# Attention shares weigh the values with the values stationary, two heads in the two column halves of TensorE

## The reference, cut to what matters

```
s = q[lo:hi] @ k[:hi].T * scale          (+ masks; fox: + forget biases; mla: + rotary part)
p = softmax(s)
o = p @ v[:hi]                            one head: 128 queries x 64 channels
y = concat(o over 16 heads) @ w_out       then residual and layer norm
```

## Time and profile before

| what | value |
|---|---|
| three runs, median (lowest to highest) | 2730.32 us (2729.82 to 2733.73) |
| the profiled execution: its span | 2727.5 us (first to last instruction; no separate time is given for it, the median is 2.8 us longer) |
| busy: PE, PEld, DVE, ACT, POOL | 97%, 83%, 37%, 51%, 72% |
| chain that ended last, by engine | PE 89%, DVE 6%, ACT 2%, DMA 1% |
| TensorE's mean granted clock | 0.991 of 2.4 GHz |

### The profile page before, as it was taken

The page is one execution under the profiler, slowest core; times in us unless marked ns, Lnnn a source line. Parts: engine busy times, 40 slices in busy tenths (PEclk is TensorE's granted clock), DMA queues, the critical chain, the costliest instruction groups (busy, mean ns, idle before and its releaser), DMA issues.

```text
span 2727.5 us, 35975 instructions
## 1 busy us (share of the span) xinstructions
PE 2651.0 (97%) x15016; PEld 2269.8 (83%) x15016; DVE 1017.6 (37%) x1695; ACT 1386.9 (51%) x1666; POOL 1972.7 (72%) x432
## 2 busy tenths in 40 slices
PE   6999989999999999999999999999999999999998
PEld 4889977899888778888888888888888888877887
DVE  6868867543212452121124311212441121244312
ACT  3754544555544555454454544544544454445543
POOL 3767764787887738878875688887658878774885
PEclk8999989999999999999999999999999999999999
DMA  8869843555554526546553455554425555443553
GB/s 331 309 230 353 311 157 108 191 213 182 200 193 175 181 88 223 188 170 216 186 197 137 160 186 194 192 192 177 155 111 199 192 193 192 179 179 115 194 192 108
DMA packets 80390, 521.78 MB, mean 191 GB/s; under 512 B 8908, under 2 KB 9292, under 8 KB 24420
## 3 DMA queue, kind: packets, MB, share of 16 engines
q1 hardware_dynamic: 72884, 492.72, 49.9%
q10 hardware_dynamic: 7344, 26.74, 2.5%
HBM read 518.38 MB, written 1.05 MB: 190 GB/s over the span
## 4 chain that ended last, share of the span: by engine, by line
PE 89%; DVE 6%; ACT 2%; DMA 1%; issue 0%; POOL 0%; SPq 0%; DVEq 0%; ACTq 0%
PE acc L555 17%; PE acc L594 17%; PE mb L532 11%; PE cb L532 11%; PE cb L507 10%; PE cb L534 6%; PE mb L534 6%; PE mb L647 2%; PE acc L872 1%; DVE hT L1875 1%; PE acc L507 1%; PE cb L833 1%; PE mb L857 1%; PE cb L647 1%; ACT whi L1184 1%; DMA raw<-in_w 1%
## 5 line engine op out<-in xcount | busy, mean ns | idle before, releaser
L2512 POOL TENSOR_TENSOR wlo<-raw,whi 128x2048 fp32r<-128x2048 f32 x428 | 1972.5, 4621 | 731.4 <-ACT whi L1184 667.3
L1184 ACT ACTIVATE whi<-raw 128x2048 fp32r<-128x2048 f32 x428 | 818.4, 1915 | 582.5 <-PE cb L532 251.3
L555 PE MATMUL acc<-whi,ARR 128*128 128x512 f32 x1312 | 366.5, 391 | 0.0
L532 PE MATMUL cb<-hT,whi 128*128 128x512 f32 x1280 | 335.4, 393 | 0.0
L532 PE MATMUL mb<-hT,whi 128*128 128x512 f32 x1280 | 334.1, 393 | 0.1
L555 PEld LDWEIGHTS acc<-whi,ARR 128*128 128x128 f32 x1312 | 245.6, 188 | 53.0 <-issue 2.9
L507 PE MATMUL cb<-hT,whi 128*128 128x256 f32 x1536 | 281.1, 285 | 0.0
L594 PE MATMUL acc<-whi,hT 128*128 128x512 f32 x960 | 270.8, 390 | 8.7 <-DVE hT L1875 7.4
L532 PEld LDWEIGHTS mb<-hT,whi 128*128 128x128 f32 x1280 | 230.2, 189 | 43.9 <-issue 3.1
L532 PEld LDWEIGHTS cb<-hT,whi 128*128 128x128 f32 x1280 | 229.6, 189 | 40.5
L1944 DVE TENSOR_TENSOR cb<-cb,AR 128x512 f32<-128x512 f32 x80 | 56.0, 700 | 552.8 <-ACT AR L1192 552.7
(11 more groups left out here) (332 smaller groups left out, 3367.6 us busy)
## 6 DMA issues: line engine op xcount, KB each, us to landing
raw<-in_w SPq DMA_DIRECT2D x436, 1024.0 KB, 4.8
AR<-in_a ACTq DMA_DIRECT2D x35, 512.0 KB, 6.2
AR<-in_a SPq DMA_DIRECT2D x29, 512.0 KB, 5.7
z<-in_a ACTq DMA_DIRECT2D x16, 512.0 KB, 6.8
gb<-in_lng SPq DMA_DIRECT2D x12, 512.0 KB, 5.7
gb<-in_lnb SPq DMA_DIRECT2D x12, 512.0 KB, 6.5
gb<-in_normg SPq DMA_DIRECT2D x8, 512.0 KB, 7.6
x<-in_x SPq DMA_DIRECT2D x1, 1024.0 KB, 8.4
```

Source lines behind the costliest of these rows:

```text
L532: ins = pe.matmul(to[j], wh[:, w], hT[:, k, :], start=k == 0, stop=k == 7)
L555: ins = pe.matmul(acc[:, 2 * t + c, 0:c1 - c0], xs[y], a[:, kk * width + c0:kk * width + c1], start=first and kk == 0 and m == 0, stop=las ...
L1184: ac.activation(whi[i % NH][:, :], raw[u % NR][:, :], ACT.Copy).then_inc(*up(s_hi, ("hi", i)))
L2512: po.tensor_tensor(wlo[i % NH][:, :], raw[(i + NADA) % NR][:, :], whi[i % NH][:, :].bitcast(F32), ALU.subtract).then_inc(*up(s_lo, ("lo", i)))
```

## The change

The stationary operand and the moving one trade places in weigh: the values of one head (128 keys x 64 channels) are loaded, and the turned shares (128 keys x 128 queries) move. The result has channels in the partitions; the two heads o = 0, 1 of a pair of items go to output partitions 0 to 63 and 64 to 127, that is, to the two column halves of the array. So weigh now takes two items at once, and the sum is already turned. The row sums are now what is turned: DVE takes reciprocals and spreads them over 64 columns a head into `OS` ("share"), PE turns that (turn_sums), ACT copies it back to `OS`, DVE multiplies the accumulator with it ("scale"), ACT writes the high part and DVE the low part ("split"). The order in tail is written anew. On PE, "scale" and "split" are nothing; on ACT and DVE they stand in the list where the list has them.

```diff
@@ -410,7 +410,10 @@
             t, h0 = order[name][i]
             same = [j for j in pv_order(name) if order[name][j][0] == t and order[name][j][1] // 8 == h0 // 8]
-            return same[-1] == i
+            return same[-2] == i
+
+        def exps_of(name, t, g):
+            return [i for i in range(16) if order[name][i][0] == t and order[name][i][1] // 8 == g]
         def steps(name):
@@ -424,21 +427,32 @@
         started = {"dsa0": 11, "dsa1": 11, "fox": 18, "mla": 9}
-        weighed_early = {"dsa0": (0, 1, 2, 3), "dsa1": (0, 1, 2, 3), "fox": (), "mla": ()}
+        weighed_early = {"dsa0": (0, 2), "dsa1": (0, 2), "fox": (), "mla": ()}
         def tail(name):
-            S, W, T = (lambda *a: [("step", i) for i in a]), (lambda *a: [("weigh", i) for i in a]), lambda t, g: [("turn", t, g)]
+            def S(*a):
+                return [("step", i) for i in a]
+
+            def W(*a):
+                return [("weigh", i) for i in a]
+
+            def R(t, g):
+                return [("share", t, g)]
+
+            def Y(t, g):
+                return [("scale", t, g), ("split", t, g)]
+
             if name == "fox":
-                pv = pv_order(name)
-                return W(*pv[:12]) + T(0, 0) + T(0, 1), T(1, 0) + W(*pv[12:]) + T(1, 1)
+                return (W(0) + R(0, 0) + W(4, 8) + R(0, 1) + Y(0, 0) + W(12) + Y(0, 1),
+                        W(2) + R(1, 0) + W(6) + Y(1, 0) + W(10) + R(1, 1) + W(14) + Y(1, 1))
             if name == "mla":
-                return (W(0, 1, 2, 3) + S(9) + W(4, 5, 6, 7) + T(0, 0) + T(0, 1),
-                        S(10) + S(11) + S(12) + W(8, 9) + S(13) + S(14) + W(10, 11) + S(15) + W(12, 13) + T(1, 0) + S(17)
-                        + W(14, 15) + T(1, 1))
-            return (S(11) + W(4, 5, 6, 7) + T(0, 0) + T(0, 1),
-                    S(12) + S(13) + W(8, 9) + S(14) + S(15) + W(10, 11) + S(17) + W(12, 13) + T(1, 0) + W(14, 15) + T(1, 1))
+                return (R(0, 0) + W(0, 2) + R(0, 1) + Y(0, 0) + S(9) + W(4, 6) + Y(0, 1),
+                        S(10) + S(11) + S(12) + W(8) + S(13) + S(14) + R(1, 0) + W(10) + Y(1, 0) + S(15) + W(12) + S(17)
+                        + R(1, 1) + W(14) + Y(1, 1))
+            return (R(0, 0) + Y(0, 0) + S(11) + W(4) + R(0, 1) + W(6) + Y(0, 1),
+                    S(12) + S(13) + W(8) + S(14) + S(15) + R(1, 0) + W(10) + Y(1, 0) + S(17) + W(12) + R(1, 1) + W(14) + Y(1, 1))
         def tensor_program(q):
@@ -863,24 +877,28 @@
                 g = h0 // 8
                 at, key = ("acc", 2 * t + g), (name, "o", t, g)
                 to = psum(at) if held.get(at) == key else claim(at, key)
-                q.wait_ge(*on(name, "turned", i))
+                for part in (i, i + 1):
+                    q.wait_ge(*on(name, "turned", part))
                 for kt in range(t + 1):
                     q.wait_ge(*on(name, "v", kt))
                 for j in range(2):
-                    hd = h0 + 2 * j
+                    c = (h0 % 8 // 2 + j) * 128
                     for kt in range(t + 1):
-                        ins = pe.matmul(to[:, hd % 8 * 64:hd % 8 * 64 + 64],
-                                        PT[name][i % len(PT[name])][:, (j * (t + 1) + kt) * 128:(j * (t + 1) + kt) * 128 + 128],
-                                        vals[name][:, kt, hd * 64:hd * 64 + 64], start=kt == 0, stop=kt == t)
-                ins.then_inc(*up(s_mm, (name, "weighed", i), *([("full", key)] if pv_last(name, i) else [])))
-
-            def turn_heads_sum(name, t, g):
-
-                to = claim(bank("mb"), (name, "ot", t, g))
-                q.wait_ge(*on(name, "osum", t, g))
+                        for o in range(2):
+                            hd, m = h0 + o + 2 * j, j * (t + 1) + kt
+                            ins = pe.matmul(to[64 * o:64 * o + 64, c:c + 128], vals[name][:, kt, hd * 64:hd * 64 + 64],
+                                            PT[name][(i + o) % len(PT[name])][:, m * 128:m * 128 + 128],
+                                            start=kt == 0, stop=kt == t)
+                ins.then_inc(*up(s_mm, (name, "weighed", i), (name, "weighed", i + 1),
+                                 *([("full", key)] if pv_last(name, i) else [])))
+
+            def turn_sums(name, t, g):
+
+                to = claim(bank("mb"), (name, "rt", t, g))
+                q.wait_ge(*on(name, "rsum", t, g))
                 for j in range(4):
                     ins = pe.transpose(to[:, j * 128:j * 128 + 128], OS[name][g][:, j * 128:j * 128 + 128], ident)
-                ins.then_inc(*up(s_mm, ("full", (name, "ot", t, g))))
+                ins.then_inc(*up(s_mm, ("full", (name, "rt", t, g))))
             def step(name, s, kind, ready):
                 scores, turns = steps(name)[s]
@@ -897,8 +915,10 @@
                             step(name, at[0], kind, ready)
                         elif what == "weigh":
                             weigh(name, at[0])
+                        elif what == "share":
+                            turn_sums(name, *at)
                         else:
-                            turn_heads_sum(name, *at)
+                            continue
                         yield
                 def out_ready(t, k):
@@ -910,7 +930,7 @@
                     pass
                 beside = parts(rest)
                 rows_units([(2 * j, 2 * j + 1) for j in range(4)], *hk, out_ready, ("sum", n), first=True, last=True,
-                           beside=beside, every=max(1, 46 // len(rest)), at_half=beside,
+                           beside=beside, every=max(1, 46 // (len(rest) - 4)), at_half=beside,
                            early=[(8, lambda: turn(n + 1, 0))] if n + 1 < LAST else [])
             hk = (lambda k: hTh[:, k, :]), (lambda k: hTl[:, k, :])
@@ -1522,10 +1542,15 @@
                         step(name, at[0])
                         if at[0] == len(steps(name)) - 1:
                             warm(ACT.Sqrt)
-                    elif what == "turn":
+                    elif what == "share":
                         t, g = at
-                        q.wait_ge(*on("full", (name, "ot", t, g)))
-                        copy(hTh[:, 4 * g:4 * g + 4, t * 128:t * 128 + 128], c3(view((name, "ot", t, g)), 4), (name, "oh", t, g))
+                        key = (name, "rt", t, g)
+                        q.wait_ge(*on("full", key))
+                        copy(OS[name][g], view(key), (name, "share", t, g), ("free", key))
+                    elif what == "split":
+                        t, g = at
+                        q.wait_ge(*on(name, "scaled", t, g))
+                        copy(hTh[:, 4 * g:4 * g + 4, t * 128:t * 128 + 128], c3(OS[name][g], 4), (name, "oh", t, g))
                 if started[name] == len(steps(name)):
                     warm(ACT.Sqrt)
@@ -2257,35 +2282,37 @@
                 for p in turns:
                     turned_share(name, p)
-            def result(name, t, g):
-
-                key, r = (name, "o", t, g), small("rsum", 32)[:, 16 * t + 8 * g:16 * t + 8 * g + 8]
-                q.wait_ge(*on("full", key))
-                dv.reciprocal(r, r).then_inc(*up(s_dv))
-                if t:
-                    q.wait_ge(*on("full", (name, "ot", 0, g)))
-                chain()
-                dv.tensor_tensor(c3(OS[name][g], 8), c3(view(key), 8), r.unsqueeze(2).broadcast_to([P, 8, 64]),
-                                 ALU.mult).then_inc(*up(s_dv, (name, "osum", t, g), ("free", key)))
-
-            def weighed(name, i):
-                if pv_last(name, i):
-                    t, h0 = order[name][i]
-                    result(name, t, h0 // 8)
-
             def finish(name):
                 before, rest = tail(name)
                 for what, *at in before + rest:
                     if what == "step":
                         step(name, at[0])
-                    elif what == "weigh":
-                        weighed(name, at[0])
-                    else:
+                    elif what == "share":
                         t, g = at
-                        key, sl = (name, "ot", t, g), slice(t * 128, t * 128 + 128)
+                        r = small("rsum", 32)[:, 16 * t + 8 * g:16 * t + 8 * g + 8]
+                        for i in exps_of(name, t, g):
+                            q.wait_ge(*on(name, "exp", i))
+                        dv.reciprocal(r, r).then_inc(*up(s_dv))
+                        if t:
+                            q.wait_ge(*on(name, "oh", 0, g))
+                        elif name != "mla":
+                            q.wait_ge(*on(name, "weighed", (8 if name == "fox" else 4) * g))
+                        chain()
+                        dv.tensor_copy(c3(OS[name][g], 8), r.unsqueeze(2).broadcast_to([P, 8, 64])).then_inc(
+                            *up(s_dv, (name, "rsum", t, g)))
+                    elif what == "scale":
+                        t, g = at
+                        key = (name, "o", t, g)
```

(13 more changed lines are left out.)

## The result

The changed kernel takes 2768.38 us (median of four runs, 2766.92 to 2769.72), the kernel before 2730.38 in runs beside it: ratio 1.0139, 95% interval 1.0125 to 1.0153. It is slower, by 38 us, on the side that was forecast, but 3.4 us above the upper end of the range and 21 us above the forecast. The profiled execution spans 2765.1 us, 37.6 more than before.

What follows compares the result with a forecast made beforehand. TensorE, busy 97% of the 2727.5 us span, was taken as the bound. Adding 10.8 us for the queues and 6.4 for the clock gave a span of 2744.7, a median of 2747.5; range 2728 to 2765.

Steps and rivals of the forecast that it cites:

- The pair: Weighing on TensorE: a load/multiply pair falls to 0.054 us with column halves side by side; 384 pairs, 20.7 us less.
- the changes of shape: Weighing on TensorE: 0.20 us on the way in and 0.20 out for each of 29 groups, 11.6 us.
- rival 1: Column halves don't run side by side: 2765 with halves in turn, 2782 with loads in the open as well; chance 0.17.
- rival 3: A pair of 64 columns is carried out in the full shape, without halves: 2753; chance 0.05.
- rival 2: Shape changes cost nothing for column halves and the clock stays at 1.00: 2729.5; chance of 2736 or below 0.18.
- Failed step 1: DVE in the attention stages: spreading copy between 0.35 and 0.69 us, taken as 0.69; low part 0.69.
- Failed step 2: Start of the output product: follows the low part of (0,0), turn 0.44 and weighing 0.83; mla starts 2.8 us later.
- forecast +3.8: dsa0: the output product starts at 988.9 where before it began at 985.09, 3.8 us later.
- Failed step 3: PE clock: four longest gaps charged with half of 3.2 us each, +6.4; bounds 0 to +11.
- Fox, the wrong sign: fox: output product starts 2.8 us earlier, +1.5 beside it, sum -1.35, with spread-sum waits of 0.8 and 0.7.
- Beside the output product of the others: dsa: weighing -2.1, waiting +2.2, last scaling's wait -0.3; mla: waits +2.85, +1.1, +1.2, -1.0, weighing -2.1.
- +10.8: Queues of all four stages, PE's gain included: +7.3 for both dsa, +4.85 mla, -1.35 fox.

Runs made afterwards that it cites:

- experiment 5: Changed kernel with the loop over the two column halves outermost, so each half does all its products of a pair of items first: 2780.37 us, one run.
- 1: Changed kernel with the spreading copy made by a DVE reduction over a unit axis: 2767.78 us, ratio 1.0143 to the kernel before.
- 2: Changed kernel with the scaled group left in its PSUM bank, high and low part read from there: 2768.44 us, ratio 1.0146 to the kernel before.
- 3: Changed kernel with both edits, spread by reduction and scaled group left in PSUM: 2769.93 us, ratio 1.0150 to the kernel before.
- 6: Kernel before with one more DVE copy, SBUF to SBUF, ahead of each scaling: 2757.58 us, ratio 1.0103.
- 7: Kernel before with one more DVE copy of the same size, but from PSUM, ahead of each scaling: 2738.39 us, ratio 1.0033.
- 4: Changed kernel with six or nine unread small products on PE ahead of most turn_sums: 2763.69 us, ratio 1.0128 to the kernel before.
- 8: Change rewritten: weighings grouped, early spreads by reduction, turns side by side, scaling into PSUM: 2729.25 us, ratio 1.0000 to the kernel before.
- 9: 8 with ACT's tile 1 values copied behind group (0,1)'s high parts and (0,0)'s sums turned earlier: 2725.01 us, ratio 0.9984 to the kernel before.
- 10: 9 with ACT also rounding its next block of weights only behind group (0,1)'s high parts: 2727.60 us, ratio 0.9991 to the kernel before.

## Why the prediction was off

**What held.** The pair cost 0.051 for a forecast 0.054; the changes of shape 0.20 and 0.20; rival 1 (halves in turn), both its forms, and rival 3 are excluded by experiment 5 and by the piece of 1.02, rival 2 (no cost of shape) by the 1.13 behind it. So the loads of a half don't wait for the products of the other half, though both use all 128 rows. The net of these, 9.1 us less work, fits the busy time (8.6 us more) if the clock took 17.7 back. A count bears this out roughly: over the whole span PE is busy for 80.7 us at the lower level, 36.2 before, and 44.5 more at half the pace are 22 us. Most of the waits stand where they were drawn: PE is idle before turn_sums(0,1) of dsa0 on the spreading copy, 4.21 us where 4.9 was forecast, and in mla before the last weighing of tile 0, 2.85 for 3.1. The 2.65 us before turn_sums(0,0) in both dsa stages were not drawn; I had PE turn that group long before ACT was free.

**Failed step 1: the price of the spreading copy and of the low part.** I priced the copy at 0.69, "between 0.35 and the 0.69 of other 512-column work", and bounded it by rows none of which is a copy within SBUF; the low part I left at 0.69 though its operand moved from PSUM to SBUF. Measured: 0.43, but 4.06, 4.06, 2.68 and 2.65 in four places, and 2.10, 2.10 and 2.28 for three low parts. The upper bound was missing, and half of the four places have the full 4.06. The working for dsa0, with the shift of 0.96 by which the changed kernel is ahead there: the turn of (0,1) was due at 987.6, so 986.6, and came at 988.8. The copy of the sums on ACT was 1.0 late (982.72 for 981.7, behind the 4.06), the low part 1.4 longer, the second spread 0.26 shorter, which is the 2.2 us.

**Failed step 2: what the output product waits for.** I let it go once the low part of (0,0) was there and group (0,1) weighed. Its first product also takes the accumulator bank that the scaling of (0,1) frees: at 991.83 it waits 0.86 us for L2308 in dsa0, and 1.52 in fox. With 0.9 for turn and weighing at half clock this completes dsa0: 2.2 + 0.9 + 0.86 is 3.9 to 4.0 later than the forecast +3.8, so the product starts 7.7 later. In mla it starts 6.3 later for a forecast 2.8.

**Failed step 3: the clock.** I charged four gaps with 3.2 us at half clock each, 13 us, for a cost of 6.4. Measured are 53 us at half clock, in which work that takes t takes 2t: some 18 to 22 us of PE's busy time by the two accounts above, and part of the idle time through longer turns. The unit was wrong: the row that I took it from the earlier trace rows shows 3 us behind one gap, and my upper bound, 11 us, is made of the same unit. But the level can stay down much longer with no further gap of that size, 10.2 us in dsa0. The trace of the kernel before shows it as well, in two stretches of earlier stages that I did not read (columns as above):

```profile
41.40:51.60 10.20, 7.34 (x29) 5.78 (x30) 9.77 (x16) 5.94 (x7) 4.75 (x2) 0.50 0.85 333
348.60:365.60 17.00, 13.18 (x59) 12.64 (x60) 7.65 (x13) 6.76 (x9) 10.00 (x3) 0.50 0.72 255
```

In the first PE was idle for 2.43 us at its start and for 1.00 at the most later, in the second for 3.65 us near its start and then 1.02 at the most. What decides between 3.4 us and 10 to 17 no run here shows.

**Fox, the wrong sign.** From the first weighing to the output product I forecast 2.8 us less; it is 11.8 us for 9.2, 2.6 more. The two waits for spread sums, 0.8 and 0.7 by forecast, are 2.88 and 2.74, and step 2 adds 1.52. Beside the product it is +2.8 for a forecast +1.5.

**Beside the output product of the others.** In mla it is 7.2 us more for a forecast 2.05, and in dsa0 2.1 more for a forecast of 0.15 less. Of the 13.6 us at half clock that mla has from 1988.1 on, 10.9 lie behind the start of its product; of the 10.2 of dsa0, 6.4.

In sum: stages +37.7 where I had +10.8 and 6.4 of clock. I can't split the 20 us between the three steps by adding them up. Experiments 1 to 3 show why: each wait taken away leaves one nearly as late behind it. What is shown is that the wait for POOL, with the clock that it costs, is worth some 19 us in the old order (6 against 7); that in the new order no edit that took it away gained anything (1 to 3), though 2 and 3 also free the bank later, so that its worth there isn't measured by itself; that giving back part of the clock is worth 3 to 5 us (4); and that order, port, clock and fewer bursts together are worth the whole (8: 39 us less with the same 384 pairs).

## What to carry to other kernels

Price a new DVE instruction by a row of the same kind with the same memories on its operands: a copy within SBUF, or an operation with two inputs there, can last as long as the POOL instruction beside it and a little more, not its own length. A broadcast can be written as a reduction over a unit axis, and a product can be left in PSUM, without that wait. A cheaper TensorE step pays only if the handovers behind it are off the path: put the turns together, early spreads first, and ACT's bulk copies behind the chain. These were tried together, so no run tells what each is worth. And take from the trace the longest stretch at half clock as well as a short one: here 3.4 us and 17 us stand in the same trace, and the bound of a forecast must hold the longer.

## What the runs showed of the hardware

- Two column halves that share all 128 rows overlap fully when their pairs alternate: 0.051 us a pair (128x64 loaded, 128 columns moved, fp32), 0.109 in one half alone. A block of eight pairs in each half lies in between, 0.082 on average ((1.51 - 0.20) / 16), because the second block starts before the first has ended (experiment 5).
- A DVE copy of 128x512 fp32 within SBUF takes 0.43 us alone, less than the 0.69 from PSUM, and up to 4.06 beside POOL, ending 0.28 us behind POOL's instruction; a reduction with the same output takes 0.69 in both cases.
- Adding work to the engine that is the bound made the kernel 3 to 5 us faster, with some 30 us at half clock in four windows where there were 53 (experiment 4).
- Behind a gap of 2.59 us the level stayed down for 3.4 us, behind one of 2.10 us at the same place for 10.3 (experiments 9 and 10, mla).
